# The odd mixer of a two-layer block, run as one stream of weight units

## The chip, the cores and the metric

The kernel runs on one core of a Trainium2 chip. The metric is device time in microseconds, from the first to the last instruction of one launch, taken as the median of several runs. The core has TensorE (PE; its weight loads are shown apart as PEld), VectorE (DVE), ScalarE (ACT), GpSimd (POOL) and the queue of SyncE (SP), which here only issues weight loads.

## The reference, cut to what matters

A block of two layers (an even and an odd mixer, each followed by a SwiGLU) and a third layer of another kind work on 256 tokens of width 2048, all in float32. The change concerns the odd mixer, which is this:

```python
def mixer_odd(x, cos, sin, w_in, conv_w, conv_b, mlstm_bi, mlstm_bf, mlstm_norm_g,
              mla_qnorm_g, mla_kvnorm_g, mla_wuq, mla_wukv, w_o):
    cq, ck, cv, ci, cf, co, mq, mkv, mkr = _split(x @ w_in, (512, 512, 1024, 4, 4, 1024, 512, 512, 64))
    qk = silu(causal_conv(concatenate([cq, ck], -1), conv_w, conv_b))      # 4 taps
    h = mlstm(q, k, cv, ci + mlstm_bi, cf + mlstm_bf)                      # 4 heads, chunks of 64 tokens
    o_c = sigmoid(co) * head_layer_norm(h, mlstm_norm_g)
    q = (rms_norm(mq, mla_qnorm_g) @ mla_wuq).reshape(B, S, 8, 128 + 64)   # latents: 512 wide
    kv = (rms_norm(mkv, mla_kvnorm_g) @ mla_wukv).reshape(B, S, 8, 128 + 128)
    o_d = causal_latent_attention(q_nope, rope(q_rope), k_nope, rope(mkr), v)
    return concatenate([o_c, o_d], -1) @ w_o                               # 2048 x 2048
```

Its result is added to x, and a layer norm follows. `mlstm` keeps a matrix state, a vector n and a running maximum per head from chunk to chunk, and divides each row by max(|q.n|, exp(-m)).

## The kernel before

Weights come in **units** of 128 x 1024 float32 (512 KB). SP loads a unit into one of 8 raw slots (L197); ACT rounds it to `weights_hi` (`unit_hi`, L214); DVE forms the rest `weights_lo` (`unit_lo`, L221); PE multiplies: twelve matmuls of 128x512 for a unit (hi*hi, lo*hi, hi*lo for two k-tiles and two token halves, L259 to L261). There are 4 slots for the split halves, so ACT splits unit u once PE has finished unit u-4. A **block** is 512 columns of a product; it accumulates in one of two pairs of PSUM banks (0,1 and 2,3), and its evacuation frees the pair. A **turn** is one PSUM bank (4 or 5, alternately) filled with four 128x128 transposes by `turn` (L328) and emptied by ACT, by DVE or by both. The engines' programs are written out by hand, each in order; a semaphore count is what one waits for in another.

The first 8 units of a stage (the "lead", `lead_mm`, L505 to L507) have their transposes of x between the units.

The odd mixer before runs in these parts, one behind the other (`upto >= 3` in each engine's program):
- x @ w_in: a lead block, six blocks in a loop, a narrow block of 72 columns (two units, `narrow_mm`, L287 to L289), a last block;
- the latents' norms, their turns, then w_uq (3 blocks of two units) and w_ukv (4 blocks of two units), evacuated in the middle of the next block's splits (`block_split(..., between)`);
- rope on DVE (L2205 to L2210), then turns of all heads;
- the attention (`att_pe`, `att_act`, `att_dve`; scores L585, turned probabilities L597, product L610) for 16 items (8 heads by 2 token halves);
- the cell: turns, the convolution on DVE (32 instructions, L2250 and L2252), the gates' rows (4 x 256, L2259 to L2271, with ACT's exponentials L1707 to L1710), the silu (L1712), the chunk states (L2696, L2286, L2288), and for eight (head, half) pairs scores and sums (L2706 to L2724 on PE, L1722 on ACT, L2304 to L2324 on DVE), then the norm and the gate (L2332 to L2341);
- eight turns of the mixed result and the product with w_o: four blocks of eight units, added to x (`residual`, L1772), then layer norm 3.

In the second mixer (the third layer), before as after, the small work already stands between units: `block_mm` and `block_split` call `c.beside()` after each unit, which calls `second_pe(v)`, `second_act(u)`, `second_dve(u)` with the unit's number. ACT and DVE do step e = u - 4 behind the split of unit u. An item of its attention is spread over four steps: scores at v (L880), scale and maximum on DVE at e = v (L928, L931), exponential on ACT at v+1 (L904), turn at v+2 (L328), copy on ACT (L912), product at v+3 (L893) and division on DVE (L938, L939).

## Time and profile before

| | |
|---|---|
| median of 3 runs | 3761.83 us (3751.89 to 3762.16) |
| the profiled execution's own time | 3755.04 us |
| its span, first to last instruction | 3753.2 us |
| PE busy, share of the span | 3526.6 us, 94% |
| DVE busy, ACT busy | 1980.5 us (53%), 1604.4 us (43%) |
| odd mixer, end of the lead to the last matmul with w_o | 1323.94 to 1806.30 us |

Times within the execution are in microseconds from the start of the span. PE counts as busy from the start of a matmul to its modelled end, at whatever clock it has: the granted clock (1.00 is 2.4 GHz, 0.50 is 1.2 GHz) must be read beside it.

### The profile page before, as it was taken

How to read it: one execution, taken by the hardware profiler on the slowest of the kernel's cores; microseconds unless marked ns; L12 is line 12 of the kernel's file. 1: busy time of each engine (PE TensorE's matmuls, PEld its weight loads, DVE VectorE, ACT ScalarE, POOL GpSimd, SP SyncE). 2: the span in 40 equal slices, each digit the busy share in tenths (PEclk: the TensorE clock that was granted, in tenths of full speed). 3: DMA queues.
4: the chain of work that ended last, by engine and by line, in shares of the span. 5: the costliest groups of instructions: out<-in, count | busy, mean ns of one | idle time of the engine just before them, and what ended most of it. 6: DMA issues, size and time to landing. Idle time of an engine off the chain costs nothing.

```text
span 3753.2 us, 43606 instructions
## 1 busy us (share of the span) xinstructions
PE 3526.6 (94%) x15810; PEld 2866.3 (76%) x15810; DVE 1980.5 (53%) x2391; ACT 1604.4 (43%) x2010; POOL 286.5 (8%) x402
## 2 busy tenths in 40 slices
PE   8999699999999898768999999999998899999997
PEld 7887578888888687546787887887887778888886
DVE  4444365555455644355657554547543655545555
ACT  4453334444444344323444444445555554444443
POOL 0000000000000000000148000200082000000000
PEclk9999799999999999858999999999999999999999
DMA  7664156656666464204665654854553556655663
GB/s 241 189 182 144 45 174 204 193 181 197 184 192 188 134 198 147 71 1 163 175 185 178 196 180 151 249 184 163 174 177 113 167 156 189 189 183 186 193 190 113
DMA packets 335156, 630.65 MB, mean 168 GB/s; under 512 B 33164, under 2 KB 35440, under 8 KB 333504
## 3 DMA queue, kind: packets, MB, share of 16 engines
q1 hardware_dynamic: 330416, 611.59, 53.0%
q0 software_dynamic: 4624, 17.51, 1.5%
q8 instruction: 73, 1.20, 0.1%
q14 instruction: 43, 0.35, 0.0%
HBM read 625.64 MB, written 2.33 MB: 167 GB/s over the span
## 4 chain that ended last, share of the span: by engine, by line
PE 88%; DVE 6%; POOL 3%; ACT 2%; issue 1%; DMA 0%; SPq 0%; ACTq 0%; DVEq 0%
PE psum L259 26%; PE psum L260 26%; PE psum L261 26%; PE psum L328 2%; DVE weights_lo L221 1%; PE psum L505 1%; PE psum L506 1%; PE psum L507 1%; POOL big L1237 1%; POOL scratch L1238 1%; PE psum L585 1%; POOL scratch L1239 1%; PE psum L610 1%; ACT weights_hi L214 0%; PE psum L2474 0%
## 5 line engine op out<-in xcount | busy, mean ns | idle before, releaser
L221 DVE TENSOR_TENSOR weights_lo<-weights_raw,weights_hi 128x1024 fp32r<-128x1024 f32 x1155 | 1420.7, 1246 | 1199.1 <-ACT weights_hi L214 1198.1
L214 ACT CAST weights_hi<-weights_raw 128x1024 fp32r<-128x1024 f32 x1155 | 1207.3, 1050 | 1623.8 <-PE psum L261 1603.1
L259 PE MATMUL psum<-weights_hi,act_hi 128*128 128x512 f32 x3232 | 1280.2, 396 | 25.4 <-DVE weights_lo L221 21.0
L261 PE MATMUL psum<-weights_hi,act_lo 128*128 128x512 f32 x3232 | 1263.9, 391 | 0.0
L260 PE MATMUL psum<-weights_lo,act_hi 128*128 128x512 f32 x3232 | 1263.3, 391 | 0.0
L259 PEld LDWEIGHTS psum<-weights_hi,act_hi 128*128 128x128 f32 x3232 | 610.0, 189 | 155.5 <-issue 23.9
L261 PEld LDWEIGHTS psum<-weights_hi,act_lo 128*128 128x128 f32 x3232 | 609.6, 189 | 129.7
L260 PEld LDWEIGHTS psum<-weights_lo,act_hi 128*128 128x128 f32 x3232 | 610.8, 189 | 122.6
L259 PE MATMUL psum<-weights_hi,hid_hi 128*128 128x512 f32 x1216 | 483.6, 398 | 16.6 <-DVE weights_lo L221 15.4
L260 PE MATMUL psum<-weights_lo,hid_hi 128*128 128x512 f32 x1216 | 476.5, 392 | 0.0
L261 PE MATMUL psum<-weights_hi,hid_lo 128*128 128x512 f32 x1216 | 475.8, 391 | 0.0
L259 PEld LDWEIGHTS psum<-weights_hi,hid_hi 128*128 128x128 f32 x1216 | 229.6, 189 | 84.4 <-DVE weights_lo L221 27.7
L261 PEld LDWEIGHTS psum<-weights_hi,hid_lo 128*128 128x128 f32 x1216 | 229.7, 189 | 49.3
L260 PEld LDWEIGHTS psum<-weights_lo,hid_hi 128*128 128x128 f32 x1216 | 229.8, 189 | 45.1
L1771 DVE TENSOR_TENSOR x<-x,psum 128x512 f32<-128x512 f32 x164 | 105.2, 683 | 130.1 <-PE psum L261 130.1
L328 PE MATMUL psum<-ident,big 128*128 128x128 f32 (+2 forms) x684 | 110.3, 291 | 63.5 <-DVE act_lo L365 14.8
L328 PEld LDWEIGHTS psum<-ident,big 128*128 128x128 f32 (+2 forms) x684 | 87.4, 149 | 89.6 <-issue 15.1
L1152 POOL DMA_DIRECT2D big<-in_ln_g x4 | 2.1, 532 | 1692.8 <-DVE big L2341 1148.5
L2029 DVE TENSOR_TENSOR big<-big,psum 128x512 f32<-128x512 f32 x44 | 28.2, 684 | 118.0 <-PE psum L261 118.0
L1771 DVE TENSOR_TENSOR big<-big,psum 128x512 f32<-128x512 f32 x58 | 37.2, 684 | 75.0 <-PE psum L261 75.0
L328 PE MATMUL psum<-ident,x 128*128 128x128 f32 x192 | 35.1, 321 | 43.8 <-DVE x L1820 18.7
L505 PE MATMUL psum<-weights_hi,act_hi 128*128 128x512 f32 x160 | 69.5, 435 | 0.0
(384 smaller groups left out, 1863.8 us busy)
## 6 DMA issues: line engine op xcount, KB each, us to landing
weights_raw<-in_ffn_wgu SPq DMA_DIRECT2D x352, 512.0 KB, 4.4
weights_raw<-in_w_ff SPq DMA_DIRECT2D x256, 512.0 KB, 4.2
weights_raw<-in_ffn_wd SPq DMA_DIRECT2D x176, 512.0 KB, 3.9
weights_raw<-in_even_w_in SPq DMA_DIRECT2D x120, 512.0 KB, 3.7
weights_raw<-in_odd_w_in SPq DMA_DIRECT2D x64, 512.0 KB, 3.7
weights_raw<-in_w_in SPq DMA_DIRECT2D x64, 512.0 KB, 3.8
weights_raw<-in_odd_w_o SPq DMA_DIRECT2D x32, 512.0 KB, 4.5
weights_raw<-in_w_out SPq DMA_DIRECT2D x32, 512.0 KB, 4.0
```

The source lines that it names most:

```text
L214: nc.scalar.copy(w_hi[:, u % SPLIT_SLOTS, :size], raw[:, u % RAW_SLOTS, :size]).then_inc(hi_ready, 1)
L221: nc.vector.tensor_tensor(w_lo[:, u % SPLIT_SLOTS, :size], raw[:, u % RAW_SLOTS, :size], w_hi[:, u % SPLIT_SLOTS, :size].bitcast(F32), ALU ...
L259: nc.tensor.matmul(o, ah, wh, start=(k + j == 0), stop=False)
L260: nc.tensor.matmul(o, ah, wl, start=False, stop=False)
L261: last = nc.tensor.matmul(o, al, wh, start=False, stop=(k + j == kts - 1))
L328: last = nc.tensor.transpose(psum[:w, 4 + t % 2, at_col:at_col + p], src, ident[:p, :p])
L505: nc.tensor.matmul(o, ah, wh, start=(u + j == 0), stop=False)
L506: nc.tensor.matmul(o, ah, wl, start=False, stop=False)
L507: last = nc.tensor.matmul(o, al, wh, start=False, stop=(2 * u + j == KT_D - 1))
L585: last = nc.tensor.matmul(flat[:, col:col + k.shape[1]], q, k, start=(i == 0), stop=(i == len(pairs) - 1))
L610: last = nc.tensor.matmul(product_of(it, n), it["pt"][:, n % 2, i * P:(i + 1) * P], it["v"][i], start=(i == 0), stop=(i == nt - 1))
L1771: return TENS(o, o, s, ALU.add)
```

## The change

The weight units of the odd mixer (112 with the lead) stay the same, in another order, and go through in one stream. Block ends (numbers of units, lead included) are in `ODD_ENDS`: the lead block now holds columns 3072.. (the end of the cell's output gate and most of the q latent), then 3584.. (the kv latent) and the narrow one, q of the cell, w_uq, w_ukv, then k of the cell (512..), its two gates and half of its output gate (2048..), v (1024.. and 1536..), the rest of the output gate (2560..), and w_o in two passes of four blocks with four units each: first rows 1024 to 2047 (the attention's half of the input), added to x by DVE at steps 83, 87, 91 and 95, then rows 0 to 1023 (the cell's half). All other work is in steps `odd_pe(v)`, `odd_act(u)` and `odd_dve(u)`, called behind each unit as in the second mixer. Attention items use the helpers of the second mixer (`item_pe`, `item_act`, `item_dve`), which lose one DVE instruction for each item (the sign is taken in the scale), in the second mixer too. Rope's halves of two heads share one turn. The latents' gains are applied on their turns (`gained_hi`, `gained_lo`), the rms factors at the evacuations. The cell's division is folded into the norm's factors. The buffers in SBUF are laid out anew; LN 3's vectors are loaded after step 90 instead of after the cell.

```diff
+            for col, cols in ((3072, BLK), (3584, BLK), (4096, 72), (0, BLK)):
+                block_load(sp, c, w, 0, KT_D, col, cols)
+            (3 blocks of w_uq, 4 of w_ukv, two units each)
+            for col in (512, 2048, 1024, 1536, 2560):
+                block_load(sp, c, w, 0, KT_D, col, BLK)
+            for row in (1024, 0):
+                for j in range(4):
+                    block_load(sp, c, A["odd_w_o"][0], row, 8, j * BLK, BLK)
...
+    ODD_ENDS = [8, 16, 18, 26, 28, 30, 32, 34, 36, 38, 40, 48, 56, 64, 72, 80, 84, 88, 92, 96]
+    def odd_taken(eng, c, e):
+        b = odd_block(c, e)
+        eng.wait_ge(acc_free[b % 2], c.freed(b))
+    def latent_item(i):
+        h, m = i // 2, i % 2
+        q, nk, r = slice(m * P, (m + 1) * P), P * (m + 1), slice(64 * (h % 2), 64 * (h % 2) + 64)
+        return {"i": i, "n": 8 + i, "sc": l_sc, "pt": l_pt, "stat": l_stat, "cols": nk,
+                "pairs": [(lqT[:, h, q], lkT[:, h, :nk]), (lqrT[r, h // 2, q], lkrT[r, :nk])],
...
         def scale():
-            nc.vector.tensor_tensor_reduce(n_sc[...], psum[:, 6, 0:256], bias, 1.0, -3e38, ALU.add, ALU.max, top)
-            dve.wait_ge(att_scaled, n + 1)
-            nc.vector.tensor_scalar(neg, top, -1.0, None, ALU.mult).then_inc(att_maxed, 1)
+            nc.vector.tensor_tensor_reduce(it["sc"][:, i % 2, :cols], psum[:, 6, 0:cols], it["add"], -it["scale"], 3e38,
+                                           ALU.add, ALU.min, least).then_inc(att_scaled, 1)
...
+        def odd_act(u):
+            e = u - 4
+            if e in (48, 65):
+                act.wait_ge(ready("ml_conv"), 1 if e == 48 else 2)
+                A_(of, of, ACT.Silu).then_inc(ready("ml_qk"), 1)
+            if e in (58, 61, 65, 70):
+                turn_take_hi(act, c, hT_hi[:, k:k + 2, :].rearrange("p k t -> p (k t)"))
+            i = e - 49
+            if 0 <= i < 16:
+                item_act(act, c, latent_item(i))[0]()
+            i = e - 50
+            if 0 <= i < 16:
+                item_act(act, c, latent_item(i))[1]()
+            if e == 58:    (Abs, Exp, Ln of the gates' rows)
+            if e == 64:    (ten small exponentials: ml_exps)
+            j = e - 76
+            if 0 <= j < 8:
+                A_(eT[:, j % 2, :], psum[:, 6 + j % 2, 0:P], ACT.Exp, scale=-1.0, bias=col6[:, m, h:h + 1])
+            j = e - 78
+            if 0 <= j < 8:
+                act_turn(act, c, nums[:, j, 0:257])
...
+        conv_at = {e: [n] for n, e in enumerate([29, 30, 31] + list(range(35, 48)))}
+        conv_at |= {51: [16, 17], 52: [18, 19], 53: [20, 21]} | {54 + n: [22 + n] for n in range(10)}
+            if e == 59:         (the gates' sums: three instructions on 4 x 256)
+            if e in (60, 61):   (two chunks' running maxima each)
+            if e == 68:         (ml_kw, the old states' factors)
+            if e in (69, 71, 73, 75):   (a head's three states)
+            if 0 <= e - 76 < 8:
+                ml_weights(e - 76, c.n["turn"])
+            if e in (83, 87, 91, 95):
+                evac_at(dve, c, e, b, lambda m, o: STT(out=x[...], in0=x[...], scalar=ALPHA, in1=o, ...))
...
+        def odd_pe(v):
+            if v in (18, 20, 22, 23):                 tiles(lqkv, ...)         # turn
+            if v in (27, 28, 49, 50):                 tiles(qkraw, ...)        # turn
+            if v in (34, 36, 38, 40):                 turn(pe, c, [qb_heads ...])
+            if v in (37, 39):                         turn(pe, c, [rq ...])
+            if 41 <= v < 45:                          turn(pe, c, [kb ...])
+            if v in (58, 61, 65, 70):                 turn(pe, c, [lqT ...])   # the attention's results
+            if v == 66:
+                pe.wait_ge(ready("ml_exps"), 1)
+                turn(pe, c, [rows[:, j, m * P:(m + 1) * P] for j in (R_A, R_W, R_E) for m in range(TT)])
+            if v in (67, 68):                         turn(pe, c, [qk ...])
+            item i: score at v = 48 + i, turn_probs at 50 + i, product at 51 + i
+            if v in (69, 71, 73, 75):                 (a head's local sums; at 69 eight columns for n)
+            j = v - 76: scores, three matmuls         j = v - 78: the sums over v and the old state
+            if v in (88, 89, 92, 93):
+                pe.wait_ge(ready("ml_out"), h // 2 + 1)
+                turn(pe, c, [nums ...])
...
+            odd_stage(c, odd_pe)
+            block_mm(pe, c, KT_D, BLK, aT_hi, aT_lo)
             narrow_mm(pe, c, 72)
             block_mm(pe, c, KT_D, BLK, aT_hi, aT_lo)
-            (turns, wait, w_uq and w_ukv; rope wait, turns; att_pe; the cell; turns; w_o)
+            all_turned()
+            for k0, n in ((0, 3), (4, 4)):
+                for _ in range(n):
+                    block_mm(pe, c, 4, BLK, hT_hi, hT_lo, k0)
+            for _ in range(5):
+                block_mm(pe, c, KT_D, BLK, aT_hi, aT_lo)
+            for t in latent_turns:
+                turn_stands(pe, t)
+            for _ in range(4):
+                block_mm(pe, c, 8, BLK, hT_hi, hT_lo)
+            all_turned()
+            c.stage(None)
+            for _ in range(4):
+                block_mm(pe, c, 8, BLK, aT_hi, aT_lo)
```

Lines in brackets or with `...` in an argument stand for code left out.

## Rows read from the trace of the kernel before

**Rows 1.** The page, parts 1 and 5: busy time and share; a line's groups, mean ns.

```profile
PE 3526.6 (94%) x15810; PEld 2866.3 (76%) x15810; DVE 1980.5 (53%) x2391; ACT 1604.4 (43%) x2010; POOL 286.5 (8%) x402
...
L221 DVE TENSOR_TENSOR weights_lo<-weights_raw,weights_hi 128x1024 fp32r<-128x1024 f32 x1155 | 1420.7, 1246 | 1199.1 <-ACT weights_hi L214 1198.1
L214 ACT CAST weights_hi<-weights_raw 128x1024 fp32r<-128x1024 f32 x1155 | 1207.3, 1050 | 1623.8 <-PE psum L261 1603.1
```

**Rows 2.** Windows: stretch, length, busy by engine, granted clock, DMA share, GB/s.

```profile
1485.00:1550.00 65.00, 48.36 (x184) 37.22 (x184) 22.13 (x24) 29.20 (x41) 0.00 (x0) 0.84 0.36 113
...
1575.00:1621.20 46.20, 35.33 (x115) 22.50 (x114) 13.25 (x63) 9.56 (x37) 0.00 (x0) 0.56 0.00 0
1621.20:1705.20 84.00, 45.02 (x151) 27.48 (x149) 58.76 (x189) 17.57 (x33) 0.00 (x0) 0.55 0.00 0
...
1717.03:1806.30 89.27, 89.27 (x384) 73.58 (x384) 47.17 (x45) 32.91 (x32) 0.00 (x0) 0.97 0.64 199
```

**Rows 3.** PE's waits from 1485 to 1720 us, the longest: total, times, longest (us).

```profile
PE psum L2684 <- ACT big L1710: 20.6, 1, 20.6
```

**Rows 4.** Timeline, DVE in the second mixer: two splits of a plain unit.

```profile
2738.37 1.24 DVE L221 TENSOR_TENSOR weights_lo<-weights_raw,weights_hi 128x1024 fp32r<-128x1024 f32 x1 [1.49 <-ACT weights_hi L214]
2741.09 1.23 DVE L221 TENSOR_TENSOR weights_lo<-weights_raw,weights_hi 128x1024 fp32r<-128x1024 f32 x1 [1.48 <-ACT weights_hi L214]
```

**Rows 5.** Timeline, PE: turns between lead units; the lead's end; w_in's end.

```profile
1308.91 0.60 PE L328 MATMUL psum<-ident,x 128*128 128x128 f32 x4
...
1312.10 0.60 PE L328 MATMUL psum<-ident,x 128*128 128x128 f32 x4
...
1323.94 0.39 PE L259 MATMUL psum<-weights_hi,act_hi 128*128 128x512 f32 x1
...
1481.92 0.29 PE L328 MATMUL psum<-ident,scratch 72*128 72x72 f32 x2
```

**Rows 6.** Timeline, PE in the second mixer: a unit with one item's steps.

```profile
2749.74 0.59 PE L880 MATMUL psum<-big,big 128*128 128x256 f32 x2
2750.17 0.38 PE L328 MATMUL psum<-ident,big 128*128 128x128 f32 x2
...
2753.60 0.59 PE L880 MATMUL psum<-big,big 128*128 128x256 f32 x2
```

**Rows 7.** Windows (as rows 2): the second mixer with its attention items.

```profile
2740.00:2760.00 20.00, 20.00 (x99) 16.39 (x98) 11.34 (x25) 12.30 (x23) 17.42 (x34) 1.00 0.63 201
```

**Rows 8.** Timeline, DVE in the cell: the same instruction of two successive pairs.

```profile
1675.42 0.29 DVE L2304 SCALAR_TENSOR_TENSOR scratch<-psum,scratch 128x128 f32<-128x128 f32 x1 [0.24 <-ACT scratch L1722]
...
1679.20 0.29 DVE L2304 SCALAR_TENSOR_TENSOR scratch<-psum,scratch 128x128 f32<-128x128 f32 x1 [0.25 <-ACT scratch L1722]
```

**Rows 9.** The chain that ended last, in the cell: start, us, what.

```profile
1654.50 7.50 PE psum L2696 x24
```

**Rows 10.** Groups by line: a convolution instruction on DVE; mean ns.

```profile
L2252 DVE SCALAR_TENSOR_TENSOR scratch<-scratch,big,scratch 128x256 f32<-128x256 f32 x24 | 9.8, 480 | 0.1
```

**Rows 11.** Timeline, ACT in the cell: first small exponential, table load, silu.

```profile
1644.46 0.35 ACT L1707 ACTIVATE big<-big,big 4x64 f32<-4x64 f32 x1 [13.00 <-DVE big L2271]
...
1646.89 1.28 ACT L1712 ACT_TABLE_LOAD   x1
1648.19 1.91 ACT L1712 ACTIVATE scratch<-scratch 128x2048 f32<-128x2048 f32 x1
```

**Rows 12.** Timeline, PE in w_ukv: a wait and the matmuls behind it.

```profile
1522.22 0.47 PE L259 MATMUL psum<-weights_hi,act_hi 128*128 128x512 f32 x1 [3.46 <-DVE weights_lo L221]
...
1523.71 0.63 PE L259 MATMUL psum<-weights_hi,act_hi 128*128 128x512 f32 x1
...
1524.99 0.63 PE L259 MATMUL psum<-weights_hi,act_hi 128*128 128x512 f32 x1
...
1527.33 0.39 PE L259 MATMUL psum<-weights_hi,act_hi 128*128 128x512 f32 x1
```

**Rows 13.** Waits from 2640 to 2960 us, second mixer: total, times, longest (us).

```profile
ACT big L1448 <- POOL smalls L1240: 12.0, 1, 12.0
```

## What the change will do to the time

> **What bounds the kernel now.** I read the page first. PE is busy for 94% of the span [rows 1]. The two splits of a unit take 1.25 us on DVE and 1.05 us on ACT [rows 1], and a plain unit passes every 2.72 us (1.48 us of DVE's time between two splits is idle) [rows 4]. So in plain stretches PE is the bound, with 1.47 us of DVE and 1.67 us of ACT to spare in each unit. Then I cut the odd mixer into windows. From 1485 to 1705 us it is something else: granted clock 0.84, 0.56 and 0.55 in the windows of the latents' products, of the attention and of the cell, and PE busy for 48 of 65, 35 of 46 and 45 of 84 us [rows 2]. "Busy" there is mostly small work at the lower clock (1.2 GHz). Nothing is loaded in the last two. PE's longest wait is 20.6 us for the exponentials of the cell's gates [rows 3], behind 32 convolution instructions on DVE. It is a chain in which each engine waits for another. With w_o (1717.03 to 1806.30) PE is busy for all of the 89.27 us [rows 2].
>
> **What is removed.** Count from the end of the lead, 1323.94 [rows 5], to the last matmul with w_o, 1806.30 [rows 2]: 482.4 us. In it stand 104 units, of which 102 are full: 102 x 2.72 = 277.4 us [rows 4]. The narrow pair: w_in's 56 full units and the two narrow ones end at 1481.92 [rows 5], so 157.98 - 56 x 2.72 = 5.7 us. Bare units: 283.1 us. The other 199.3 us are small work, waits and lower clock. The change moves that work between the units. What of PE's own part is left stays on the path, because PE is the bound; it is now paid at the full clock if the clock stays up.
>
> **What PE's small work costs between units.** (a) 28 turns of four transposes (steps 18, 20, 22, 23; 27, 28; 34, 36 to 45 without 45; 49, 50; 58, 61, 65, 70; 67, 68; 88, 89, 92, 93). In the lead a unit with such a turn takes 1312.10 - 1308.91 = 3.19 us [rows 5], so a turn costs 0.48 us: 13.4 us. (b) 14 single transposes (steps 19, 45, 57, 66) at a quarter of that: 1.7 us. (c) 16 attention items. The second mixer shows an item between units: 3.86 us from score to score, 1.14 over a plain unit, of which the 128x256 score is 0.43 [rows 6]. A latent item of the second token half has one more score product of that size (rope): 1.57 us. One of the first half has half the columns everywhere: 0.78 us. 8 x 2.35 = 18.8 us. (d) The cell's scores and sums: a pair now takes 1679.20 - 1675.42 = 3.78 us [rows 8] with PE nearly full at clock 0.55 [rows 2]; at the full clock half, 1.89 us. Eight pairs: 15.1 us. (e) The states: 7.5 us at the lower clock [rows 9], 3.8 at the full one, and twelve tiny products (for n and the old factors), estimated at 0.12 each as in (b): 5.2 us. Sum: 54.2 us. Bounds: a quarter less where a matmul of few columns overlaps its neighbours, a quarter more where it doesn't: 41 to 68. I take 54; the terms from rows 5 and 6 are measured at the full clock and make up 34 of it.
>
> **Will DVE and ACT keep up?** DVE: in steps 54 to 63 it has a split (1.25), one convolution instruction (0.48) [rows 10], and an item's scale, maximum and division (two such instructions and two tiny ones, 1.0): 2.7 us in a unit that takes PE 3.9. In the cell's steps: 1.25 + 0.95 + 0.7 = 2.9 in 4.6. ACT has 1.05 + 0.85 and 1.05 + 0.75. So on the mean both are under PE everywhere. The question is latency: PE's queue is in order, and each wait in a step holds every unit behind it. A step's partners start about 1.3 us (ACT) and 2.4 us (DVE) after PE's unit, for ACT first splits the next unit. I went through the steps with these durations and found four tight places.
> - Step 66. From the end of unit 64: ACT splits (1.2), exponential 15 and copy 14 (0.8), then ten small exponentials, 2.4 us (1644.46 to 1646.89) [rows 11]: done at 4.4. Then the next split 1.0, the silu's table load 1.28 and the silu, half the 1.91 of before [rows 11], the latent turn's rounding 0.6: 8.3; DVE's part of it 0.7: 9.0. PE is there after step 64 (0.5), a unit, step 65 (0.9) and a unit: 6.8. Its next turn needs the bank of that turn, so it waits 2.2 us.
> - Steps 59 to 63. DVE has the gates' rows on top (1.5, 1.3, 1.3 us, and 0.7 for a turn), 1.5 us more than PE's time over three units; about 0.8 us come through.
> - Step 69. DVE scales eight tiles of k and takes the old factors (4.0 us after unit 68, PE is there at 3.4): 0.7 us.
> - Steps 51 to 53, 76: 0.1 us each.
> That is 4.1 us. To it comes the clock: behind a wait of 3.46 us the matmuls ran at the lower level from 1523.71 to 1527.33 [rows 12], half of which, 1.8 us, is lost; I add that once. Total 6 us. Bounds: 0 (the margins elsewhere are 0.5 us and more, and the second mixer ran a stretch with items in which PE was never idle, at clock 1.00 [rows 7]) to 45 (below).
>
> **Edits at nothing.** The four extra evacuations to x (8 x 0.68 us of DVE, steps 83 to 95) and the sigmoid, norm factors and gate (steps 84 to 90) lie in units without items and go 20 us before they are needed (pass 2 starts at unit 96). The cell's convolution, 32 instructions, is spread over single units; without that cover it is at most 32 x 0.48, 15 us. LN 3's vectors (2 MB by POOL) now load among the weights, at about 0.64 of the DMA's time [rows 2], some 50 us ahead of their use; the weight slots hold 8 units. SP waits for nothing new: it keeps being released by the splits. POOL only moves that load and three tiny gathers, long before. The dropped DVE instruction of each of the second mixer's 24 items saves 0.15 us off the path: PE is the bound there [rows 7].
>
> **The page on tables.** Table loads on ACT rise from 8 to 11, one of them in the tight step 66. The load's row is 1.28 us, and the silu starts 1.30 us after it [rows 11]. The Trainium skill (ScalarE: Activation LUTs, Table sets: the hidden batching unit) says to batch calls by set, which the change does not do, and puts a switch at about 2.66 us with a drain. By that the wait at step 66 would be 1.4 us longer and the sum 7 instead of 6; the trace shows no such drain.
>
> **Sum.** 283.1 + 54.2 + 6 = 343.3 us in place of 482.4: a gain of 139 us. Against the profiled execution's own 3755.04 us that gives 3616. The median of the runs is 6.8 us above that execution, so by the median 3623; I forecast 3620, between the two. What stands around (the lead, layer norm 3, the later stages) keeps its shape and only comes earlier; late next is the second mixer's own wait for POOL's recurrence, 12 us [rows 13], which starts from its own stage and doesn't grow.
>
> **Rivals.**
> - The steps' latencies come through (the waits take the place of the old chain). Speaking for it: one bank of two is released late, and the waits form chains over three engines; in the second mixer ACT waits 12.0 us for another engine in one step [rows 13]. Against: the same item pattern runs with PE always busy [rows 7]. Price: 0.7 us for each of 16 items, 1.3 us for each of 8 pairs and each of 11 table loads: 36 us, and three times the clock's 1.8: 41 us instead of 6. Time 3655, in a range of 3635 to 3680.
> - PE's small work is cheaper than (a) to (e), 41 us, and nothing waits: 3620 - 13 - 6 = 3601 us.
> - Slower: the granted clock stays at its lower level through the stream, because small matmuls and short waits stand between the units. Place: all units from step 27 on. A unit at the lower level takes 12 x 0.43 = 5.1 us (three matmuls from 1523.71 to 1524.99) [rows 12], 2.4 more, and the small work doubles. All 102 units: 245 + 54, so 3620 + 299 = 3919. It decides from 139/(2.4 + 0.5) = 48 such units. Against: clock 1.00 with items between units [rows 7]; for: 0.55 in the cell now [rows 2]. In a sentence of its own: the Trainium skill (TensorE: Matmul & The Clock Gate, A second HAM failure mode: psum-queue depth-cycling) describes such an oscillation between groups of matmuls; rows 7 speak against it here.
> - The change doesn't do what it says: the cell's chain (states, eight pairs, norm, gate) can't be hidden because pass 2 needs its end. There are units up to 96 for it; if half of the cell's 84 us [rows 2] still stood bare, 3662; if all, 3704.
>
> **Chances.** Forecast (3605 to 3635) 0.70; latencies or part of the cell left bare (3635 to 3710) 0.20; cheaper (under 3605) 0.06; slower by the clock 0.02; something that ends within 0.3% or slower by other ways 0.02. 0.3% (11 us) is about what a measurement of this kernel can tell from no change. The range 3600 to 3650 holds the forecast, half of the cheaper case and about half of the late one: 0.82. Faster 0.96, same 0.01, slower 0.03.
>
> **What would show it.** No window without loads between 1485 and 1660; granted clock 1.00 nearly throughout; the last matmul with w_o near 1667; PE's wait at step 66 (for `hid_lo`) near 2 us; table loads 11. Wrong would be: a lower clock in windows of the cell's steps; waits of PE for ACT's exponentials or for DVE's `att_done` at each item; a unit with a full latent item well over 4.3 us.

## The result and the profile after

The changed kernel takes 3624.61 us in the median (3619.14 to 3625.15), the kernel before, run beside it, 3761.99 us (3751.89 to 3762.65): a ratio of 0.9638, 95% interval [0.9619, 0.9656], so 137 us or 3.6% less. The forecast was 3620 us in a range of 3600 to 3650. The profiled execution took 3624.08 us, with a span of 3622.2.

The page of the kernel after, parts 1 and 2: busy time, granted clock in 40 slices, DMA share in 40 slices.

```profile
PE 3477.5 (96%) x15818; PEld 2837.3 (78%) x15818; DVE 1951.2 (54%) x2307; ACT 1618.7 (45%) x2052; POOL 288.8 (8%) x402
...
PEclk9999799999999999999999999999999999999998
DMA  7665056665655555446655656655544456566663
```

The same two rows of the page before:

```profile
PEclk9999799999999999858999999999999999999999
DMA  7664156656666464204665654854553556655663
```

PE is busy for 49 us less than in [rows 1] and the span is 131.0 us shorter: the other 82 us were idle time of PE. The slices of clock 8 and 5 in the middle of the row are gone, and so are the slices there with the DMA engines at 2 and 0.

PE's timeline after: the first matmul behind the lead, and the last one with w_o.

```profile
1323.06 0.39 PE L259 MATMUL psum<-weights_hi,act_hi 128*128 128x512 f32 x1
...
1673.83 0.39 PE L261 MATMUL psum<-weights_hi,act_lo 128*128 128x512 f32 x1
```

From the first start to one pitch (0.23 us) behind the last start are 351.0 us. I call this the stretch. Before it was 482.4 [rows 2, 5]; the forecast was 343.3. The stretch gained 131.4 us and the whole span 131.0, so the rest of the kernel is as long as before, and everything below is about the stretch. I quote the stretch of each run beside its time, because single times scatter by 3 to 6 us. It is read from one profiled execution of each kernel. Two such executions of the changed kernel agree within 0.2 us once the microseconds at the lower clock are taken out, and differ by 3.2 with them ("Three repairs").

Windows after: the stretch; attention; step 65 to the old states' factors; the cell (columns as in rows 2).

```profile
1323.00:1675.00 352.00, 349.39 (x1671) 278.32 (x1670) 207.28 (x386) 184.67 (x290) 1.10 (x2) 1.00 0.53 162
1444.00:1516.00 72.00, 72.00 (x357) 56.25 (x357) 44.82 (x123) 41.88 (x92) 0.00 (x0) 1.00 0.44 126
1516.00:1538.00 22.00, 20.17 (x111) 16.32 (x111) 11.72 (x27) 8.13 (x10) 0.00 (x0) 1.00 0.45 140
...
1546.00:1600.00 54.00, 54.00 (x247) 38.26 (x246) 30.66 (x69) 24.05 (x35) 0.00 (x0) 1.00 0.39 122
```

PE has work for 349.4 of 352 us at clock 1.00, where the windows of [rows 2] had 0.84, 0.56 and 0.55, and PE busy for half to three quarters. VectorE is busy for 0.62 of the attention's window and ScalarE for 0.58. In place of the 20.6 us of [rows 3], PE's list of waits in this stretch has one line (unit pauses under about 0.2 us are not in it):

```profile
PE psum L329 <- DVE hid_lo L346: 1.8, 1, 1.8
```

So the waits are 1.8 us, the 104 bare units 283.1 by the prediction's count, and PE's small work takes the rest, 66 us, where 54.2 was forecast. The experiments ask three things: whether the gain comes from what the prediction named (cover, clock, the cell behind pass 1), how close the order is to waits, and why the small work is dearer.

### The profile page after: what moved, and what is told of

Same layout as the page of the kernel before. It is cut to its first block, busy times and chain, and to the rows that moved or that the text cites. A ratio compares the mean times of both kernels' runs of the same rounds, so it can differ in the third digit from the quotient of the medians.

```text
span 3622.2 us, 43342 instructions
## 1 busy us (share of the span) xinstructions
PE 3477.5 (96%) x15818; PEld 2837.3 (78%) x15818; DVE 1951.2 (54%) x2307; ACT 1618.7 (45%) x2052; POOL 288.8 (8%) x402
## 4 chain that ended last, share of the span: by engine, by line
PE 90%; DVE 4%; POOL 3%; ACT 1%; issue 1%; DMA 0%; SPq 0%; DVEq 0%; ACTq 0%
PE psum L259 27%; PE psum L261 27%; PE psum L260 27%; PE psum L329 2%; POOL big L1274 1%; PE psum L510 1%; PE psum L512 1%; PE psum L511 1%; DVE weights_lo L221 1%; POOL scratch L1276 1%; POOL scratch L1275 1%; PE psum L918 0%; DVE x L1889 0%; PE psum L2754 0%; DVE x L1938 0%
## 5 line engine op out<-in xcount | busy, mean ns | idle before, releaser
L259 PE MATMUL psum<-weights_hi,act_hi 128*128 128x512 f32 x3112 | 1234.2, 397 | 12.8 <-DVE weights_lo L221 8.4
L261 PE MATMUL psum<-weights_hi,act_lo 128*128 128x512 f32 x3112 | 1216.4, 391 | 0.0
L260 PE MATMUL psum<-weights_lo,act_hi 128*128 128x512 f32 x3112 | 1215.2, 390 | 0.0
L259 PEld LDWEIGHTS psum<-weights_hi,act_hi 128*128 128x128 f32 x3112 | 586.7, 189 | 135.5 <-issue 15.2
L261 PEld LDWEIGHTS psum<-weights_hi,act_lo 128*128 128x128 f32 x3112 | 586.1, 188 | 124.7
L260 PEld LDWEIGHTS psum<-weights_lo,act_hi 128*128 128x128 f32 x3112 | 586.9, 189 | 116.9
L259 PE MATMUL psum<-weights_hi,hid_hi 128*128 128x512 f32 x1336 | 532.6, 399 | 16.6 <-DVE weights_lo L221 15.3
L260 PE MATMUL psum<-weights_lo,hid_hi 128*128 128x512 f32 x1336 | 523.2, 392 | 0.0
L261 PE MATMUL psum<-weights_hi,hid_lo 128*128 128x512 f32 x1336 | 523.1, 392 | 0.0
L261 PEld LDWEIGHTS psum<-weights_hi,hid_lo 128*128 128x128 f32 x1336 | 252.5, 189 | 54.4
L510 PE MATMUL psum<-weights_hi,act_hi 128*128 128x512 f32 x160 | 68.9, 430 | 0.0
```

What stands on the lines that cost most here:

```text
L259: nc.tensor.matmul(o, ah, wh, start=(k + j == 0), stop=False)
L260: nc.tensor.matmul(o, ah, wl, start=False, stop=False)
L261: last = nc.tensor.matmul(o, al, wh, start=False, stop=(k + j == kts - 1))
L510: nc.tensor.matmul(o, ah, wh, start=(u + j == 0), stop=False)
```

## Experiments

All are edits of the changed kernel unless said otherwise. A stretch that is so many us "behind" is that much longer than its 351.0 us.

### The wait at step 66

```
-            if e in (48, 65):          (ACT: silu of q, of k)
+            if e == 48:
...
             item_act(...)              (the items' operations)
+            if e == 65:
+                (silu of k, here)
```

> The changed kernel, with the silu of k (step 65 on ACT) behind the latent turn and the copy of item 15 instead of ahead of them. Theory (what PE waits for at step 66 is a bank that ACT and DVE release late because the table load and the silu stand ahead of it): PE's wait of 1.8 us for hid_lo goes, no other comes, and the stretch from the lead's end to the last matmul with w_o falls from 351.2 to 349.4 us. Rival (the silu itself is the late work, so the wait only moves): a wait of about 1 us or more at step 67 for the silu, and a gain under 0.8 us.

The stretch was 349.3 us, the single time 3619.6. ScalarE's timeline in the kernel after, before the edit, shows what step 66 waited for:

```profile
1515.53 0.40 ACT L1502 ACTIVATE big<-big 4x256 f32<-4x256 f32 x1
...
1515.93 1.03 ACT L214 CAST weights_hi<-weights_raw 128x1024 fp32r<-128x1024 f32 x1
1516.98 1.28 ACT L1470 ACT_TABLE_LOAD   x1
1518.27 1.06 ACT L1470 ACTIVATE big<-big 128x1024 f32<-128x1024 f32 x1
1519.24 0.57 ACT L338 CAST hid_hi<-psum 128x512 fp32r<-128x512 f32 x1
```

The exponentials, the split, the table load, the silu and the rounding stand in one row, as the prediction laid them out. PE's turn in the edited kernel:

```profile
1515.13 0.50 PE L329 MATMUL psum<-ident,big 4*128 4x4 f32 x6 [0.19 <-DVE hid_lo L346]
```

The wait fell from 1.8 to 0.2 us, and the stretch by the same 1.7. The cause of the one wait is shown.

### Is it the cover that keeps the clock up?

All sixteen attention items in one burst at step 48, in the same order among themselves, with no weight unit between them; ScalarE and VectorE do their part in a burst too.

```
-            i = v - 48
-            if 0 <= i < 16: item_pe(...)[0]()     (and [1] at v - 50, [2] at v - 51)
+            if v == 48:
+                for s in range(19):
+                    for part, i in ((0, s), (1, s - 2), (2, s - 3)):
+                        if 0 <= i < 16: item_pe(pe, c, latent_item(i))[part]()
```

> Undoes one part: all 16 attention items run at step 48, one behind the other with no unit between, everything else as in the changed kernel. Theory (between units the items cost PE only its own 25 us; bare, each waits for DVE and ACT, and PE's clock falls): 16 x 3.2 us = 51 us bare, so 24 to 30 us slower than the changed kernel, granted clock near 0.5 to 0.6 in the burst. Rival (what counted was only taking the old waits out, the pace of an item is PE's either way and the clock stays up): 16 x 2 = 32 us, under 10 us slower, clock 1.00.

3655.63 us, ratio 0.9727 [0.9711, 0.9744]; the stretch 380.6, 29.6 behind (1.7 of it is lower clock at step 69, last section). Windows of this kernel: before the burst, its first and its second half.

```profile
1420.00:1443.00 23.00, 23.00 (x111) 18.88 (x111) 11.81 (x15) 11.28 (x16) 0.00 (x0) 1.00 0.58 165
1443.00:1470.00 27.00, 23.33 (x71) 14.85 (x69) 8.31 (x33) 12.03 (x30) 0.00 (x0) 0.60 0.18 53
1470.00:1496.00 26.00, 23.79 (x72) 15.76 (x72) 6.95 (x33) 6.70 (x23) 0.00 (x0) 0.50 0.00 1
```

Its waits of PE in the burst:

```profile
PE psum L918 <- DVE big L962: 4.3, 9, 2.0
PE psum L931 <- DVE big L968: 1.6, 3, 0.7
```

The burst took 51.8 us, against about 25 for the same products between units. Only 6 us of it are waits. PE is shown as busy for 47 of 53 us, but at the lower clock (1.2 GHz) for all but the first microseconds. So most of what bare attention costs is not idle time: it is the clock. It fell at 1448, behind PE's first two pauses in the burst (2.0 and 0.5 us). Taking the weight units away brought both the pauses and the missing large matmuls, and the run does not tell which of the two lowered the clock; that the mix with weight units holds it at 1.00 here is shown. The rival, that the clock falls with any mix of small products and units, is refuted by the windows after.

### Is it the two passes that hide the cell's end?

The output product in one pass over all sixteen rows of tiles, so that no weight unit is left to cover the cell's last fourteen steps.

```
-            for row in (1024, 0):
-                for j in range(4): block_load(sp, c, A["odd_w_o"][0], row, 8, j * BLK, BLK)
+            for j in range(4):
+                block_load(sp, c, A["odd_w_o"][0], 0, KT_D, j * BLK, BLK)
...
+            for v in range(80, 94): odd_pe(v)          (bare; DVE and ACT: 84 to 97)
+            (then the product, 16 tiles a block)
```

> Undoes one part: the product with w_o is again one pass of four blocks of eight units, and steps 80 to 93 (six of the eight score steps' rest, the norm, the gate, the turns) run one behind the other without units between. Theory (the cell's last third is hidden by the first pass): before, the same work from the fourth pair to the split of the last turn took 1679 to 1715, 35 us; PE's own part of it between units is 13 us, so this kernel is 20 to 28 us slower than the changed one (the ratio to the kernel before about 0.970), with a lower granted clock in the bare stretch. Rival (two passes bring little because the cell's end is short and PE does the same work): under 6 us slower.

3641.84 us, ratio 0.9693 [0.9677, 0.9709], 17 us over the changed kernel's median (21 by the two ratios, since the kernel before was 5 us faster beside this one); the stretch 367.2, 16.2 behind. Windows and waits of this kernel:

```profile
1580.00:1600.00 20.00, 8.57 (x39) 5.35 (x38) 10.55 (x36) 14.28 (x25) 1.09 (x2) 0.70 0.05 7
1600.00:1620.00 20.00, 17.72 (x73) 14.62 (x73) 7.86 (x9) 6.11 (x8) 0.00 (x0) 0.87 0.57 200
```

```profile
PE psum L329 <- DVE big L2194: 11.4, 2, 6.6
...
PE psum L2975 <- DVE act_lo L366: 2.3, 1, 2.3
```

13.7 us of it are PE's waits for the gated result of the cell and for its turned tiles, and the rest fits the lower clock in these two windows. I had expected 20 to 28, so the size was overrated; the rival (under 6) is refuted. Of the change's 131 us, the second pass carries about 16, and the mixing of the attention about 28. The other 87 us (the latents' products, the turns, the convolution and the first part of the cell, now between units) no run takes apart.

### How much room have ScalarE and VectorE?

ScalarE makes each weight unit's high half twice at the sixteen units 53 to 68 (an identical second copy); in a second kernel VectorE makes the low half twice at the same units.

```
+        if (the odd stage) and 53 <= u - c.base < 69:
+            act_link(c, nc.scalar.copy(w_hi[...], raw[...]))
```

```
+        if (the odd stage) and 53 <= u - c.base < 69:
+            dve_link(c, nc.vector.tensor_tensor(w_lo[...], raw[...], w_hi[...], ALU.subtract))
```

> The changed kernel, but ScalarE makes the high half of each weight unit twice at sixteen units of the odd layer (53 to 68), about 1.1 us more in each 4.2 us period. Theory: the stretch is TensorE's, and ScalarE, busy for about 0.6 of the period there, has room: the stretch grows by at most 3 us, all of it as a longer wait at the steps where ScalarE also has the silu or the small exponentials (the 1.8 us at step 66). Rival, the three engines stand in a tight chain and each small delay of ScalarE comes through: 16 x 0.5 or more, 8 to 18 us, in waits of TensorE on the low half of the weights or on turned tiles at many steps.

> The changed kernel, but VectorE makes the low half of each weight unit twice at the same sixteen units, about 1.1 us more of VectorE's time a period. Its busy share at 1455 to 1520 us is 0.6 to 0.68. Theory: at the steps of attention the period is 4.2 us and VectorE has about 2.8 of it, so that 3.9 still fits, and only steps that bring the cell's scans besides (59 to 63, 66) give waits: 3 to 10 us more in the stretch. Rival, VectorE's own order with its waits on other engines leaves no such room: 16 x 1.1 = 18 us or more, spread over all sixteen steps.

The first gave 3628.23 us and a stretch of 357.1, the second 3630.77 and 357.7. Each of these two stretches holds 1.7 us of lower clock, the first behind the wait at step 66 (1520 to 1530, granted clock 0.83), the second at step 69 (1540 to 1550, 0.84), which is a matter of its own (last section). Without it, 16.8 us of added work on ScalarE cost 4.4 us, and 19.6 us on VectorE cost 5.0. PE's waits with ScalarE's double work:

```profile
PE psum L331 <- DVE hid_lo L348: 2.4, 1, 2.4
PE psum L920 <- DVE big L964: 1.6, 5, 0.6
...
PE psum L933 <- DVE big L970: 0.3, 1, 0.3
```

(Two lines are added above these functions, so L920 here is L918 of after.) The tight chain is refuted for both: three quarters of the added work vanished. For VectorE the theory (3 to 10) held: 1.9 us of its waits stand at steps 59 and 61 to 63, 0.6 at steps 52 and 54. For ScalarE the theory (at most 3, and at step 66) did not: only 0.6 of it shows at step 66, 1.6 in waits of the items' scores at steps 52, 54, 59, 60 and 62, and 0.3 in one for a result. The remaining 1.9 us stand in pauses too short for the list. ScalarE's split comes ahead of the item's exponential, and the exponential is a link of the item's chain, which I take for the reason. Its room is in the mean, not in each step.

### What does a small product cost?

Six equal fp32 products (output unused) at each of six steps that have no small work, then a second set that varies the neighbours.

```
+            sizes = {29: (P, 256), 30: (P, 128), 31: (64, 128), 32: (64, 256), 33: (P, 1), 35: (4, 128)}
+            if v in sizes:
+                rows_, cols_ = sizes[v]
+                for _ in range(6):
+                    MM(psum[:, 6, 0:cols_], ident[0:rows_, :], mla_mask[0:rows_, 0:cols_], start=True, stop=True)
```

> The changed kernel with six additional float32 matmuls behind each of six units that have no step of their own on PE (units 29 to 33 and 35), written to an unused bank: 128 rows x 256 columns, 128x128, 64x128, 64x256, 128 rows x 1 column, 4x128. Theory A, the one of the forecast (a small matmul costs its columns, 0.43 us at 256): six cost 2.6, 1.3, 1.3, 2.6, under 0.2 and 1.3 us. Theory B (each of the two passes of a float32 matmul has a weight load in front of it that nothing covers, about 0.05 to 0.1 us a pass): six cost about 3.2, 2.0, 2.0, 3.2, 1.2 and 2.0 us, whatever the rows.

PE's timeline, the groups of six (form: rows x columns of the moving operand):

```profile
1388.92 2.75 PE L2621 MATMUL psum<-big,ident 128*128 128x256 f32 x12
...
1394.29 1.50 PE L2621 MATMUL psum<-big,ident 128*128 128x128 f32 x12
...
1398.45 1.60 PE L2621 MATMUL psum<-big,ident 64*128 64x128 f32 x12
...
1402.93 2.85 PE L2621 MATMUL psum<-big,ident 64*128 64x256 f32 x12
...
1408.57 1.39 PE L2621 MATMUL psum<-big,ident 128*128 128x1 f32 x12
...
1412.69 0.60 PE L329 MATMUL psum<-ident,big 128*128 128x128 f32 x4
```

From one group's start to the next, less a unit of 2.72, six products cost 2.65, 1.44, 1.76, 2.92 and 1.40 us: each 0.44, 0.24, 0.29, 0.49 and 0.23. The six with four rows took 1.66 (1415.99 to 1420.37), 0.28 each. Theory A was near for 256 columns and wrong for one (under 0.2 for six); theory B was near for one and wrong for 256 (3.2). Columns count from 128 to 256. Below that they don't: one column costs as much as 128. Each fp32 product is two entries of the trace (x12 for six), each with its own weight load, while a transpose is one entry; four transposes cost 0.49. 256 columns at 0.44 us are what the Trainium skill (FP8 and Floating Point Precision, TensorE Precision Notes) leads to: true fp32 takes four passes through the array, so 4 x 256 columns at the full clock would be 0.43, an estimate from that page. The same rule gives 0.21 for 128 columns and next to nothing for one, and there the trace differs.

These prices did not add up to an attention item, whose rows have a product of 64 rows beside one of 128. Hence the second set, with single products, pairs, and rows that change within a group.

```
+            sizes = {29: [(P, P, 6), (P, P, 7)] * 3, 30: [(P, P, 6)], 31: [(P, P, 6), (64, P, 6)],
+                     32: [(P, P, 6), (P, P, 6)], 33: [(P, P, 6), (64, P, 6)] * 3,
+                     35: [(P, 256, 6), (64, 256, 6)] * 3, 46: [(P, 1, 6)], 47: [(P, 256, 6)]}
...
```

> The changed kernel with extra fp32 products (output unused) at eight steps of the odd layer that have no small work of their own but, at most, turns: six 128x128 that change the PSUM bank each time (step 29), one (step 30), one with 128 rows and one with 64 (31), two alike (32), six that change between 128 and 64 rows (33), six 128x256 that change between 128 and 64 rows (35), one of one column (46), one 128x256 (47). The first run of sizes had 0.24 us for each of six equal 128x128, 0.29 at 64 rows, 0.44 and 0.49 for 256 columns. Theory A, a fixed cost of about 0.09 us at each change of kind (weight unit to small product, small product to the next kind, back to the unit), which six equal products spread thin: one alone costs 0.35 to 0.45, a pair that changes the rows about 0.65, the six that change rows 2.0 to 2.2 against 1.5 to 1.6 without such a cost. Theory B, the price of a product is that of its own shape, wherever it stands: one alone 0.24, the pair 0.53, two alike 0.48, the changing six 1.59, the six of 256 columns 2.79, one of one column 0.23, one of 256 columns 0.44. The six that change the bank: 1.44 if the bank is of no account.

```profile
1386.18 0.38 PE L2621 MATMUL psum<-big,ident 128*128 128x128 f32 x2
...
1389.17 0.80 PE L2621 MATMUL psum<-big,ident 128*128 128x128 f32 x4
...
1392.75 0.60 PE L2621 MATMUL psum<-big,ident 128*128 128x128 f32 x4
...
1395.93 2.46 PE L2621 MATMUL psum<-big,ident 128*128 128x128 f32 x12
...
1401.18 0.60 PE L329 MATMUL psum<-ident,big 128*128 128x128 f32 x4
...
1404.39 3.73 PE L2621 MATMUL psum<-big,ident 128*128 128x256 f32 x12
```

In the same way: one product alone 0.27, two alike 0.46, the pair of 128 and 64 rows 0.86, the six that change 2.53, the six of 256 columns that change 3.80 (to 1410.91). So neither theory was right. The place of a product does not matter (0.27 alone, as B said; one of one column 0.25, one of 256 columns 0.48), nor does the bank: six that change it took 4.08 us with their unit (1382.10 to 1386.18), 1.36. What costs is a **change of the number of rows**, from the unit's 128 to fewer or back. A group of 64 rows has two changes, where it is entered and where it is left: six of 64 rows are 0.32 us (128 columns) and 0.27 (256) dearer than six of 128, six of four rows 0.22. The pair is 0.40 dearer than two alike, for two changes. The alternating sixes have six: 2.53 - 1.44 and 3.80 - 2.65 are 0.18 and 0.19 for each. That is 0.11 to 0.20 us a change, and I took 0.16. On weight loads the Trainium skill (TensorE: Matmul & The Clock Gate, Step-by-step: what each phase is for) says that they are pulled ahead of running matmuls when the row groups don't conflict or when they go to the background weight buffer, and that the row count doesn't matter for their time. The second half agrees (every weight load of the two sets took 0.18 to 0.19 us, with 4, 64 or 128 rows); that the pull-ahead fails at a change of rows would explain the price, but no row here shows it as such.

### The same price inside the attention

The rope half of the scores left out: the sixteen products of 64 rows.

```
-                "pairs": [(lqT[:, h, q], lkT[:, h, :nk]), (lqrT[r, h // 2, q], lkrT[r, :nk])],
+                "pairs": [(lqT[:, h, q], lkT[:, h, :nk])],
```

> The changed kernel with the rope half of the latent scores left out: sixteen products with 64 rows, eight of 128 columns and eight of 256, are not made, so the output is another. If the small products of attention cost what they cost in rows of equal ones (0.29 and 0.49 us), the stretch from the lead's end to the last output product falls by 8 x 0.78 = 6.2 us; priced by columns as in the prediction (1.53 ns a column) by 4.7; with a fixed cost for each change of kind of about 0.1 us more, by 7 to 8. The waits of TensorE in the stretch (1.8 us, at step 66) stay in every theory.

3615.77 us and a stretch of 342.9, which is 8.15 us shorter. The group of small products of a long item shrank from 1.57 us to 0.79 (first small product to next weight matmul), that of a short item from 1.26 to 0.82 at one step (1473.54): 1.22 a pair, 9.8 in all. With the row changes, 0.57 + 0.77 = 1.34 a pair is expected, without them 0.68 to 0.78. At four other steps the short group took 0.99 to 1.00. So about 1.6 us of the gain came back as pauses of PE, of which the list has 0.5:

```profile
PE psum L918 <- DVE big L962: 0.5, 2, 0.3
```

At 3.65 to 3.87 us a step instead of 4.1 to 4.4, the items' chain begins to be late. The 8.15 us lie just above the theory with a cost for each change (7 to 8) and well above the other two (6.2 and 4.7). I took this as support for the price of a change, and a warning on what can be gained.

### Three repairs, beside the changed kernel

All four ran on one chip. First the changed kernel once more:

> The changed kernel as it is, beside the next three on one chip. The same as before: 3619 to 3626 us, the stretch from the lead's end to the last output product 351.0 us within 0.5, one wait of 1.8 us in it.

3625.36 us (3620.87 to 3628.06), ratio 0.9653 [0.9639, 0.9666]. The stretch was 354.2, not 351.0 within 0.5. The wait at step 66 was the same 1.8 us, and the 3.2 us more are clock. The granted clock fell twice, for 3.4 us each time: from 1523.3, 1.8 us behind the end of the wait, and from 1537.0, at the end of step 69's group of small products, where PE had not paused. Each time costs 1.7 us; without them the stretch is 350.8. Windows of this run, then the first two of after:

```profile
1520.00:1525.00 5.00, 3.54 (x18) 3.03 (x19) 2.95 (x7) 1.80 (x4) 0.00 (x0) 0.84 0.53 130
1525.00:1530.00 5.00, 5.00 (x22) 3.96 (x21) 1.89 (x4) 1.05 (x1) 0.00 (x0) 0.82 0.22 83
...
1535.00:1540.00 5.00, 5.00 (x25) 4.00 (x25) 2.88 (x7) 0.65 (x1) 0.00 (x0) 0.71 0.40 145
1540.00:1545.00 5.00, 5.00 (x23) 3.80 (x22) 1.83 (x2) 1.53 (x2) 0.00 (x0) 0.95 0.03 11
```

```profile
1520.00:1525.00 5.00, 4.33 (x27) 3.77 (x28) 2.78 (x7) 1.33 (x3) 0.00 (x0) 1.00 0.54 171
1525.00:1530.00 5.00, 5.00 (x29) 4.11 (x28) 3.29 (x6) 1.78 (x2) 0.00 (x0) 1.00 0.41 123
```

**Silu late and no products of one column.**

```
-                if h == 0:
-                    b = next_turn()
-                    for k in range(8):
-                        last = local(psum[:, b, k:k + 1], k // 4 * 2, slice(256, 257), k % 4)
-                    last.then_inc(turned, 1)
-                local(psum[:, 6, 0:256], 0, slice(0, 256), h)
-                local(psum[:, 6, 256:512], 2, slice(0, 256), h)
+                b = next_turn()
+                local(psum[:, 6, 0:257], 0, slice(0, 257), h)
                 local(psum[:, 7, 0:257], 1, ...)
+                local(psum[:, b, 0:257], 2, slice(0, 257), h).then_inc(turned, 1)
```

> The changed kernel with two small things shortened: the second silu goes behind the item's operations on ScalarE (1.7 us of the wait at step 66), and the eight products of one column at step 69 go, because the states' third product is made with its 257th column into a bank of the turns. A product of one column was measured at 0.23 to 0.25 us, as much as one of 128, so their end is worth 1.8 us, less a wider product at four steps. Theory: the stretch falls by 3.2 to 3.6 us, the time by as much (ratio to the changed kernel 0.9991). Rival, columns alone count: eight columns are worth 0.1 us, and the stretch falls by 1.7 to 1.8.

3623.13 us, ratio 0.9649 [0.9636, 0.9662]; the stretch 347.9, 3.1 less than 351.0. Step 69's group in after and here:

```profile
1532.12 2.91 PE L2646 MATMUL psum<-big,big 64*128 64x1 f32 x22
```

```profile
1531.11 1.13 PE L2644 MATMUL psum<-big,big 64*128 64x257 f32 x6
```

From this group's start to the next, less a unit, step 69 takes 2.98 us in after and 1.24 here: the eight products of one column took 1.7 us of PE's time, and the rival by columns (0.1) is refuted. The stretch fell a little less than the 3.2 to 3.6 forecast. The times of the two kernels can't be told apart by their intervals; the stretches without lower clock can (347.9 against 351.0 and 350.8), one execution for this kernel.

**Rope keys with zeros.** The second score product gets 128 rows; the number of products and their columns stay.

```
-    lkrT = big(10528, [P, TOK])
+    lkrT = [big(10528, [P, TOK]), big(14616, [P, TOK])]
...
-                "pairs": [..., (lqrT[r, h // 2, q], lkrT[r, :nk])],
+                "pairs": [..., (lqrT[:, h // 2, q], lkrT[h % 2][:, :nk])],
...
-                act_turn(act, c, lkrT[:])
+                (zeros in rows 64 to 127 of the first and 0 to 63 of the second; the other halves from the turn)
```

> The changed kernel, but the rope keys stand twice, once with zeros in the lower and once in the upper 64 rows, so that the second product of each score has 128 rows as all others. The same number of products with the same columns; ScalarE has three small operations more at step 45. Theory, the change of the row count is what costs (0.16 us each time, from the row of six changing products against six equal ones): sixteen items with two changes each, 16 x 0.33 = 5.2 us less in the stretch. Rival, the latent items are limited by their chain through ScalarE and VectorE, and what TensorE saves comes back as short waits, as part of it did when the rope products were left out (8.15 of 9.8): 3 us or less.

3620.18 us, ratio 0.9643 [0.963, 0.9657]; the stretch 345.8, 5.2 less. The item's groups fell from 1.57 and 1.26 us to 1.22 and 0.92. A long item's group here, with the same columns and twice the rows in one product:

```profile
1457.79 1.02 PE L918 MATMUL psum<-big,big 128*128 128x256 f32 x4
1458.65 0.38 PE L329 MATMUL psum<-ident,big 128*128 128x128 f32 x2
1458.87 0.39 PE L931 MATMUL psum<-big,big 128*128 128x128 f32 x2
```

5.2 us were forecast from the 0.16 us of a change, and 5.2 came, 0.16 for each of 32. The rival (3 or less) is refuted; there is no new wait in the list. Whether the number of rows counts, or which rows of the array are used (odd heads had rows 64 to 127), no run tells apart.

**All of it, and the four-row products of the cell.**

```
-    head_row = big(14104, [4, 4, P])
-    rows = big(17072, [4, 8, TOK])
+    head_row = big(14104, [P, 4, P])                  (zero but in row h)
+    rows_all = big(17072, [P, 8, TOK])
+    rows = rows_all[0:4]
...
-                MM(o[:, 0:128], head_row[:, h, :], rows[:, R_M, t], start=True, stop=True)
+                MM(o[:, 0:128], head_row[:, h, :], rows_all[:, R_M, t], start=True, stop=True)
```

> Both of these together, and the two products of four rows in each cell pair made with 128 rows (the head's selector stands with zeros in the other rows), eight pairs. Theory of the row changes: 3.4 + 5.2 + 8 x 0.33 = 2.6, in sum 11.2 us less than the changed kernel in the stretch, time about 3613. Rival, the four-row products cost by something else than the change of rows (then they are as dear with 128 rows): 8.6. Shortfall in the attention as in the run before: 9.

3611.41 us (3609.69 to 3613.67), ratio 0.9621 [0.9608, 0.9634], which does not touch the interval of the changed kernel on the same chip. The stretch was 339.5: 11.5 less than 351.0, where 11.2 was forecast. The first products of two successive pairs of the cell in after, and here:

```profile
1571.24 0.48 PE L2663 MATMUL psum<-big,big 4*128 4x128 f32 x2
1571.57 0.38 PE L2664 MATMUL psum<-big,big 4*128 4x128 f32 x2
...
1576.26 0.48 PE L2663 MATMUL psum<-big,big 4*128 4x128 f32 x2
```

```profile
1561.92 0.38 PE L2665 MATMUL psum<-big,big 128*128 128x128 f32 x2
1562.13 0.39 PE L2666 MATMUL psum<-big,big 128*128 128x128 f32 x2
...
1566.55 0.38 PE L2665 MATMUL psum<-big,big 128*128 128x128 f32 x2
```

A step with a pair went from 5.02 to 4.63 us, with 32 times as many rows in two of its products: 3.1 us over eight pairs. The rival (8.6, four-row products dear for another reason) and the shortfall (9) are refuted. The median is 14 us under the changed kernel's. Lower clock behind steps 66 and 69, which this run did not have, could make up the 2.5 us beyond the stretch; that is not shown.

## Why the prediction was right, point by point

- **What bounds the stretch.** Right: PE works for all but the 1.8 us of the one wait. The bare units (283.1) are not contradicted anywhere.
- **Waits and clock, 6 us.** Step 66 was forecast at 2.2 us from ScalarE's row of operations and measured at 1.8; moving one of them removed it. The small ones (steps 59 to 63, 69, 51 to 53, 76: 1.9 us) did not appear. The clock's 1.8 us behind the wait did not appear in the profile of after; in that of its repetition 1.7 did. The term was right as a risk and not as a constant. The other 1.7 us of the repetition, at step 69, no term had.
- **PE's small work, 54.2 us: the term that was mis-sized.** It measured 66. Turns: 13.8 us, forecast (a) 13.4. Attention (c): a pair of items costs 8.48 us in two units (1455.18 to 1463.66), 3.04 over the units, about 25 in all where 18.8 stood; the unit with the long item took 4.39 us, the short one 4.09. (The sign that the prediction had set, "well over 4.3", did not come; the short item, priced at half the long one, was where it was furthest off.) The cell (d): 5.02 us a unit, 2.30 over it, 18.4 where 15.1 stood. States (e): 1.26 for step 68, 2.98 for step 69 and three times 1.28, 8.1 where 5.2 stood. The step that failed is of one kind in (c), (d) and (e): the price of a small product was taken by its columns (or halved from rows at the lower clock), and a tiny one at a transpose's 0.12 us, from (b). What the runs showed in its place: changes of the row count cost 5.2 us in the attention and 3.1 in the cell, by the padded kernels, and by the same price 0.3 at the four-row products of step 68. A tiny fp32 product costs 0.21 to 0.23, about twice 0.12; it is two entries with two weight loads where a transpose is one, which fits. The twelve add 1.2. In the states' twelve wide products no change of rows shows, though they have 64 rows: three of them cost 1.24 to 1.28 us, less than 3 x 0.44, and why is open. There the halving failed: they cost 0.62 us each at clock 0.50 [rows 9] and 0.43 at 1.00, which is 1.4 us more than the prediction's 3.8. Together 11.2 of the 12 us. Rows 6, from which the item was priced, have no product of 64 rows in them, so they could not show it. The bounds of 41 to 68 held 66.
- **Will ScalarE and VectorE keep up.** Right in the mean, and the doubled work shows by how much: 5 of 20 us came through. The margin I had put at each step of the attention was too generous for ScalarE.
- **Edits at nothing.** Nothing of them shows: the second mixer and the other stages are as long as before, and no wait for a slot or a load is in PE's list.
- **Tables.** ScalarE loads 11 tables in the stretch, as forecast, each of 1.28 us. By the longer switch of the Trainium skill (ScalarE: Activation LUTs, What ACT_TABLE_LOAD costs: about 1.28 us of load and 1.38 of drain) the wait at step 66 would have been 1.4 us longer than by the rows; at 1.8 us it was shorter than either, and the silu starts 1.29 us after the load does.
- **Rivals.** Latencies (41 us) refuted by the list of waits; cheaper small work refuted, it was dearer; the lower clock refuted with units between, and shown without them (0.50 to 0.60, 28 us); the cell's end left bare refuted, its price measured at 16.
- **The sum.** 283.1 + 66 + 1.8 = 351 against 343.3. The 12 us too little in small work and the 4 us too much in waits partly cancelled, which is the first piece of luck. The second is the choice of 3620: the sum itself gave 3616 against the profiled execution, which then took 3624.08. The 4 us added on account of the median were not needed, for the median after is 0.5 us over the profiled execution and not 6.8. So the forecast ended 4.6 us under the median, where the sum was 8 us off.

## What to carry to other kernels

Where PE is the bound and another stage runs bare with small products, put those products between weight units: here 82 of the 131 us were idle time that filled, and the other 49 were busy time, mostly at the lower clock. It needs that the helpers' work fits the steps in the mean, and that their order at the fullest step is gone through by hand. Price a small fp32 product from a row of its own shape; then look for products with fewer rows between products with 128, and try 128 rows with zeros, which cost nothing in PE's time and saved 0.33 to 0.39 us for each such place here. Not every such place need pay: the states' products with 64 rows were no dearer than their columns. Gather products of one column into a wider one.

## What the runs showed of the hardware that I had not expected

- A change of the row count between successive products cost 0.11 to 0.20 us at the full clock (0.16 over the 32 changes in the attention); fp32 products of 4, 64 and 128 rows were otherwise alike. The states' three products with 64 rows and 257 columns (1.24 us together) did not show it.
- A small fp32 product cost 0.23 to 0.25 us for 1 column, 0.24 to 0.27 for 128, 0.44 to 0.48 for 256.
- The granted clock can fall for 3.4 us, at a cost of 1.7, and it is not the same in each execution. It did so at two places. Behind the end of the wait at step 66, by 0.6 to 1.8 us: in four of nine profiles with a wait of 1.3 to 2.4 us, in none of four with 0.2 or less. At step 69, 2.6 to 2.8 us into its group of small products, where PE does not pause: in three of eleven profiles with the products of one column, in none of the two without. One execution had both. The two kernels without the wait and without those products had neither; with so few profiles, that this removes the risk is likely but not shown.
